# First weight chunk by single contraction columns, and the input by column pairs, at the head of a two-layer trunk

## What is computed

```python
def swiglu(x, w_gate, w_up, w_down):
    return (jax.nn.silu(x @ w_gate) * (x @ w_up)) @ w_down

def reference(x, ...):
    for l in range(DEPTH):
        x = layer_norm(ALPHA * x + 0.5 * swiglu(x, ffn1_w_gate[l], ffn1_w_up[l], ffn1_w_down[l]), ln1_g[l], ln1_b[l])
        mix = hybrid_mixer(x, w_in[l], ...)
        x = layer_norm(ALPHA * x + mix, ln2_g[l], ln2_b[l])
        x = layer_norm(ALPHA * x + 0.5 * swiglu(x, ffn2_w_gate[l], ffn2_w_up[l], ffn2_w_down[l]), ln3_g[l], ln3_b[l])
    return x
```

## Time and profile before

| | |
|---|---|
| median of 3 runs | 1088.04 us (1086.88 to 1088.79) |
| span of the profiled execution, first to last instruction | 1085.7 us |
| PE busy | 1073.1 us, 99% of the span |
| DVE busy | 768.2 us, 71% |
| ACT busy | 579.6 us, 53% |
| mean DMA rate over the span | 208 to 209 GB/s |

### The profile page before, as it was taken

One profiled execution on the slowest core, in us unless ns is written; L12 is line 12 of the kernel. 1 busy time (PEld: TensorE's weight loads), 2 busy tenths in 40 slices (PEclk: granted clock), 3 DMA queues, 4 the chain that ended last, 5 costly groups with the idle time before them and its releaser, 6 DMA issues.

```text
span 1085.7 us, 14631 instructions
## 1 busy us (share of the span) xinstructions
PE 1073.1 (99%) x5377; PEld 892.3 (82%) x5377; DVE 768.2 (71%) x764; ACT 579.6 (53%) x641; POOL 136.0 (13%) x137
## 2 busy tenths in 40 slices
PE   8999999999999999999999999999999999999996
PEld 6888888898888788888888888879978888888885
DVE  5756557789979775555779675666999787755556
ACT  5755554767554544444466565547774546444441
POOL 1497000000000000000007960000000000000000
PEclk9999999999999999999999999999999999999999
DMA  8877689355556477768648777675455674877770
GB/s 284 268 231 245 218 265 233 100 186 174 177 180 208 140 260 252 229 215 272 229 138 250 217 257 236 227 199 173 139 165 158 198 265 136 257 223 232 235 232 39
DMA packets 192369, 226.37 MB, mean 209 GB/s; under 512 B 31540, under 2 KB 157128, under 8 KB 192328
## 3 DMA queue, kind: packets, MB, share of 16 engines
q1 hardware_dynamic: 192328, 225.83, 65.7%
HBM read 214.26 MB, written 11.53 MB: 208 GB/s over the span
## 4 chain that ended last, share of the span: by engine, by line
PE 95%; DMA 2%; DVE 1%; SPq 1%; issue 1%; ACT 0%; POOLq 0%; DVEq 0%; POOL 0%
PE ps L572 25%; PE ps L549 18%; PE ps L551 18%; PE ps L550 18%; PE ps L533 2%; PE ps L534 2%; PE ps L535 2%; PE ps L920 1%; PE ps L922 1%; PE ps L921 1%; PE ps L587 1%; DMA raw<-in_ffn_w_up 1%; DMA raw<-in_w_in 1%; PE ps L850 1%; DMA tp<-in_ln_b 0%
## 5 line engine op out<-in xcount | busy, mean ns | idle before, releaser
L1387 DVE TENSOR_TENSOR w_lo<-raw,w_hi 128x2048 fp32r<-128x2048 f32 x173 | 403.7, 2338 | 171.1 <-ACT w_hi L1004 170.3
L1004 ACT CAST w_hi<-raw 128x2048 fp32r<-128x2048 f32 x173 | 330.1, 1911 | 174.5 <-PE ps L572 82.3
L549 PE MATMUL ps<-w_hi,xT 128*128 128x512 f32 x848 | 331.9, 391 | 0.4 <-DVE w_lo L1387 0.2
L551 PE MATMUL ps<-w_hi,xT 128*128 128x512 f32 x848 | 330.2, 389 | 0.0
L550 PE MATMUL ps<-w_lo,xT 128*128 128x512 f32 x848 | 330.2, 389 | 0.0
L549 PEld LDWEIGHTS ps<-w_hi,xT 128*128 128x128 f32 x848 | 159.2, 188 | 36.1 <-issue 2.4
L551 PEld LDWEIGHTS ps<-w_hi,xT 128*128 128x128 f32 x848 | 159.2, 188 | 33.2
L550 PEld LDWEIGHTS ps<-w_lo,xT 128*128 128x128 f32 x848 | 159.2, 188 | 32.6
L572 PE MATMUL ps<-w_hi,rows_hi 128*128 128x512 f32 x416 | 133.7, 393 | 0.0
L572 PE MATMUL ps<-w_hi,rows_lo 128*128 128x512 f32 x416 | 132.3, 390 | 0.0
L572 PE MATMUL ps<-w_lo,rows_hi 128*128 128x512 f32 x416 | 132.1, 390 | 0.0
(11 more groups left out here) (227 smaller groups left out, 1126.1 us busy)
## 6 DMA issues: line engine op xcount, KB each, us to landing
raw<-in_ffn_w_down SPq DMA_DIRECT2D x44, 1024.0 KB, 6.0
raw<-in_ffn_w_gate SPq DMA_DIRECT2D x86, 512.0 KB, 4.0
raw<-in_ffn_w_up SPq DMA_DIRECT2D x86, 512.0 KB, 5.1
raw<-in_w_in SPq DMA_DIRECT2D x30, 1024.0 KB, 5.1
hid_dram<-qT SPq DMA_DIRECT2D x160, 64.0 KB, 2.4
qT<-hid_dram SPq DMA_DIRECT2D x40, 256.0 KB, 2.7
raw<-in_w_out SPq DMA_DIRECT2D x8, 1024.0 KB, 5.0
raw<-in_w_in SPq DMA_DIRECT2D x8, 512.0 KB, 5.2
```

What stands on the lines that cost most here:

```text
L549: mm(o, xT[:, c, 0, tok], h, start=c == UPPER_FIRST[0], stop=False, skip_group_check=True)
L551: return mm(o, xT[:, c, 1, tok], h, start=False, stop=c == UPPER_FIRST[-1], skip_group_check=True)
L1004: nc.scalar.copy(w_hi[s][:, :], raw[s][:, :]).then_inc(hi_made.sem, 1)
L1387: tt(w_lo[s][:, :], raw[s][:, :], f32(w_hi[s][:, :]), ALU.subtract).then_inc(lo_made.sem, 1)
```

## The change

The input x is loaded in four pieces of two contraction columns: columns 4 and 5 of each token tile by themselves (load_rows), and the pairs 6 and 7, 0 and 1, 2 and 3 for both tiles at once (load_pair). The weights of chunks 0 and 1 come as eight columns, each with two transfers (gate and up, 128 KB each) and, but for the last of each chunk, a semaphore of its own. SP issues them in the order x 4-5 (two), column 5, x pair 1, columns 6 and 7, x pair 2, columns 0 and 1, x pair 3, columns 2 and 3; column 4 is issued by ACT ahead of its table load. ACT's casts and DVE's rests are made for one column or one pair at a time. PE makes the products of both tiles for one column after the other, and turns each pair of x one column ahead of the first product that needs it. The number of products is the same; five zero products stand at the start instead of six, and one instead of three behind the first turn. What follows chunk 1 is unchanged on every engine.

```diff
--- before.py
+++ after.py
@@ -199,8 +199,8 @@
             return ctx.enter_context(nc.semaphore(name))
 
         x_upper = [sem(f"x_upper{t}") for t in range(NT)]
-        x_lower = sem("x_lower")
-        first_landed, second_landed = sem("first_landed"), sem("second_landed")
+        x_pair = [None] + [sem(f"x_pair{p}") for p in (1, 2, 3)]
+        column_landed = {c: sem(f"column_landed{c}") for c in (4, 5, 6, 0, 1, 2)}
         third_hi, third_lo = sem("third_hi"), sem("third_lo")
         first_hi, first_lo = sem("first_hi"), sem("first_lo")
         small_landed, out_stored = sem("small_landed"), sem("out_stored")
@@ -231,7 +231,7 @@
         var_made = Events(sem("var_made"), 3 * NT)
         rstd_made = Events(sem("rstd_made"), 3 * NT)
         xn_made = Events(sem("xn_made"), 3 * 4)
-        tp_made = Events(sem("tp_made"), 3 * NT, before=NT)
+        tp_made = Events(sem("tp_made"), 3 * NT, before=3)
         tp_upper = Events(sem("tp_upper"), 3 * NT, before=NT)
         xTf_dve = Events(sem("xTf_dve"), 3 * 2)
         xTf_act = Events(sem("xTf_act"), 3 * 6)
@@ -304,25 +304,31 @@
 
             return slot[:, :].rearrange("p (c n) -> p c n", c=4)
 
+        def first_column(c):
+
+            for i, w in enumerate((ffn1_w_gate, ffn1_w_up)):
+                yield paired(raw[c < 4])[:, c % 4, i * 256:i * 256 + 256], w[0, c * P:c * P + P, 0:256]
+
         block = ctx.enter_context(nc.Block())
 
 
         @block.sync
         def _(sp):
-            first = [w[0].rearrange("(c p) n -> p c n", p=P) for w in (ffn1_w_gate, ffn1_w_up)]
-
-            def first_columns_of(c0, n, slot):
-
-                for i in range(2):
-                    yield (paired(raw[slot])[:, c0 % 4:c0 % 4 + n, i * 256:i * 256 + 256], first[i][:, c0:c0 + n, 0:256])
-
-            def load_upper(t):
-                sp.dma_start(xtok[:, t, D // 2:D], x[0, t * P:t * P + P, D // 2:D]).then_inc(x_upper[t], 16)
-
-            load_upper(0)
-            for dst, src in first_columns_of(4, 2, 0):
-                sp.dma_start(dst, src).then_inc(first_landed, 16)
-            load_upper(1)
+            def load_rows(t):
+                sp.dma_start(xtok[:, t, D // 2:D // 2 + 2 * P], x[0, t * P:t * P + P, D // 2:D // 2 + 2 * P]
+                             ).then_inc(x_upper[t], 16)
+
+            def load_pair(p):
+                n = slice(PAIRS[p][0] * P, PAIRS[p][1] * P + P)
+                sp.dma_start(xtok[:, :, n], x[0].rearrange("(t p) d -> p t d", p=P)[:, :, n]).then_inc(x_pair[p], 16)
+
+            def load_column(c):
+                for dst, src in first_column(c):
+                    sp.dma_start(dst, src).then_inc(column_landed[c], 16)
+
+            load_rows(0)
+            load_rows(1)
+            load_column(5)
             sp.sem_inc(lo_made.sem, SLOTS)
             sp.sem_inc(used.sem, SLOTS)
             def load(l, k, parts, slot=None):
@@ -367,12 +373,15 @@
 
                 k0 = FFN0[f]
                 if l == 0 and f == 0:
-                    load(l, k0, lambda r: first_columns_of(6, 2, 0))
-                    sp.dma_start(xtok[:, :, 0:D // 2], x[0].rearrange("(t p) d -> p t d", p=P)[:, :, 0:D // 2]
-                                 ).then_inc(x_lower, 16)
-                    for dst, src in first_columns_of(0, 2, 1):
-                        sp.dma_start(dst, src).then_inc(second_landed, 16)
-                    load(l, k0 + 1, lambda r: first_columns_of(2, 2, 1))
+                    load_pair(1)
+                    load_column(6)
+                    load(l, k0, lambda r: first_column(7))
+                    load_pair(2)
+                    load_column(0)
+                    load_column(1)
+                    load_pair(3)
+                    load_column(2)
+                    load(l, k0 + 1, lambda r: first_column(3))
                 else:
                     load(l, k0, gate_up(w_gate, w_up, l, 1, 0))
                     load(l, k0 + 1, gate_up(w_gate, w_up, l, 0, 0))
@@ -611,49 +620,63 @@
                     for _ in range(n):
                         mm(ps[:, 1, :], zero_b[:, 0:P], zero_b[:, :], start=True, stop=True, skip_group_check=True)
 
-                def turn(t, upper):
-
-                    for c in range(4):
-                        k = 4 * upper + c
-                        last = nc.tensor.transpose(ps[:, 6 - 2 * t + upper, c * P:c * P + P],
-                                                   xtok[:, t, k * P:k * P + P], ident[:, :])
-                    last.then_inc((tp_upper if upper else tp_made).sem, 1)
+                def turn_rows(t):
+
+                    pe.wait_ge(x_upper[t], 16)
+                    for n, c in enumerate(PAIRS[0]):
+                        last = nc.tensor.transpose(ps[:, 7 - 2 * t, n * P:n * P + P], xtok[:, t, c * P:c * P + P],
+                                                   ident[:, :])
+                    last.then_inc(tp_upper.sem, 1)
+
+                def turn_pair(p):
+
+                    pe.wait_ge(x_pair[p], 16)
+                    for n, c in enumerate(PAIRS[p]):
+                        for t in range(NT):
+                            at = n * SEQ + t * P
+                            last = nc.tensor.transpose(ps[:, (0, 6, 4, 7)[p], at:at + P], xtok[:, t, c * P:c * P + P],
+                                                       ident[:, :])
+                    last.then_inc(tp_made.sem, 1)
+
+                def both_tiles(c):
+
+                    hi, lo = (first_w_hi, first_w_lo) if c > 3 else (w_hi[0], w_lo[0])
+                    for t in range(NT):
+                        last = gate_up(hi, lo, t, c, t)
+                    return last
 
                 pe.wait_ge(zero_made, 1)
-                zeros(6)
+                zeros(5)
                 pe.wait_ge(ident_made, 1)
-                pe.wait_ge(x_upper[0], 16)
-                turn(0, 1)
-                zeros(3)
-                pe.wait_ge(x_upper[1], 16)
-                turn(1, 1)
+                turn_rows(0)
+                zeros(1)
+                turn_rows(1)
                 zeros(2)
+                pe.wait_ge(x_lo.sem, 1)
+                pe.wait_ge(first_lo, 1)
+                gate_up(first_w_hi, first_w_lo, 0, 4, 0)
                 pe.wait_ge(x_lo.sem, 2)
-                for c in (4, 5):
-                    pe.wait_ge(first_lo, c - 3)
-                    gate_up(first_w_hi, first_w_lo, 0, c, 0)
+                gate_up(first_w_hi, first_w_lo, 1, 4, 1)
+                turn_pair(1)
+                pe.wait_ge(first_lo, 2)
+                both_tiles(5)
                 pe.wait_ge(x_lo.sem, 4)
-                for c in (4, 5):
-                    gate_up(first_w_hi, first_w_lo, 1, c, 1)
-                pe.wait_ge(x_lower, 16)
-                turn(0, 0)
-                turn(1, 0)
                 pe.wait_ge(first_lo, 3)
-                for c in (6, 7):
-                    if c == 7:
-                        take(0, 0)
-                    for t in range(NT):
-                        last = gate_up(first_w_hi, first_w_lo, t, c, t)
-                last.then_inc(used.sem, 1)
+                both_tiles(6)
+                turn_pair(2)
+                take(0, 0)
+                both_tiles(7).then_inc(used.sem, 1)
+                pe.wait_ge(x_lo.sem, 6)
+                pe.wait_ge(first_lo, 4)
+                both_tiles(0)
+                turn_pair(3)
                 pe.wait_ge(second_lo.sem, second_lo.at(0, 0))
-                for upper in range(2):
-                    if upper:
-                        take(0, 1)
-                    for t in range(NT):
-                        pe.wait_ge(x_lo.sem, 6 + 2 * t)
-                        for c in (2 * upper, 2 * upper + 1):
-                            last = gate_up(w_hi[0], w_lo[0], t, c, t)
-                last.then_inc(used.sem, 1)
+                both_tiles(1)
+                pe.wait_ge(x_lo.sem, 8)
+                pe.wait_ge(first_lo, 5)
+                both_tiles(2)
+                take(0, 1)
+                both_tiles(3).then_inc(used.sem, 1)
 
             def third_of_input():
 
@@ -1118,28 +1141,38 @@
 
             def turn_input():
 
...
+                def rows_hi_(t):
+                    sc_.wait_ge(tp_upper.sem, t + 1)
+                    nc.scalar.copy(xT[:, 4:6, 0, t * P:t * P + P],
+                                   ps[:, 7 - 2 * t, 0:SEQ].rearrange("p (c n) -> p c n", c=2)).then_inc(x_hi.sem, 1)
+
+                def pair_hi(p):
+                    sc_.wait_ge(tp_made.sem, p)
+                    nc.scalar.copy(xT[:, PAIRS[p][0]:PAIRS[p][1] + 1, 0, :],
+                                   ps[:, (0, 6, 4, 7)[p], :].rearrange("p (c n) -> p c n", c=2)).then_inc(x_hi.sem, 2)
+
+                def column_hi(c, made, landed_, n):
+                    sc_.wait_ge(landed_, n)
+                    hi = first_w_hi if c > 3 else w_hi[0]
+                    nc.scalar.copy(paired(hi)[:, c % 4, :], paired(raw[c < 4])[:, c % 4, :]).then_inc(made, 1)
+
```

(46 more changed lines are left out.)

40 lines of the change are left out of this document (removed).

## The result

The changed kernel takes 1093.87 us (median of 6 runs, 1092.16 to 1096.14); the kernel before, run beside it, 1087.57 (1086.16 to 1090.10). The ratio is 1.0057, with a 95% interval of 1.0047 to 1.0067. Six more runs of the same program on another chip gave 1094.51 against 1088.75, 1.0053 (1.0036 to 1.0071). The forecast, 1090.7 with a range up to 1092.5, had the sign and the first part of the mechanism, but less than half of the size (+2.6 of +6.3 us).

A forecast was written before the change was run, and what follows sets the result against it. PE bounds the kernel (95% of the chain), so only the head matters, decided by lo_made of the second chunk. PE resuming at 28.28 instead of 25.64 gives +2.64 on 1088.04, so 1090.7 us; range 1088.4 to 1092.5.

The forecast's parts named there:

- First product: PE's first real product at the head: at 5.80 instead of 7.05, a gain of 1.25 us.
- column 4: Head transfers: x's first two pieces and column 4 of both weights landed at 4.4, with 4.0 and 5.0 as ends.
- its own sign: What the changed profile should show at the head: first product at 5.4 to 6.4.
- The gaps: PE stands 0.93 us at each of three x pairs, 2.8 in all, with one period of 4.30.
- Transfers hidden by the gaps: SP's 19 transfers up to column 3 instead of 11: last lands at 12.3 to 15.7, ACT asks at 17.7.
- lo_made and the down-chunk's load: Second chunk's rest on DVE made at 19.27 against 15.41; the down-load queued behind it on SP at 19.36.
- fourth chunk: PE goes on there at 28.28 instead of 25.64, +2.64 us, through norm rows landing at 25.62.
- The hidden rows' round trip through memory moves by about as much as PE, and had 0.9 us to spare: Behind the fourth chunk's start: the trip shifts along with PE; no cost of its own was added.
- 1: Norm rows land early, by 24.75, so PE's arrival decides: +1.6 to +1.8, 1089.7; chance 0.20.
- 2: No gap at the pairs: ACT and DVE turn one around within PE's 1.9 us; +0.3, 1088.4; chance 0.13.
- 3: Transfers bind the head: at 170 GB/s column 3 lands near 20.5; +5.2, 1093.3; chance 0.05.
- 4: Clock falls: gaps or fewer zero products leave the first 12 products slow; 2.4 more, 1093.1; chance 0.04.

The follow-up runs named there:

- Large transfers alone: Changed kernel with the transfers of before (x in three pieces, weights two columns at a time, all on SP); 1095.88 us, ratio 1.0055.
- only the late load: Kernel before, with SP holding the down-chunk's load until PE has used chunk 1; 1090.46 us, ratio 1.0032.
- all three edits: Changed kernel with weight column ahead of x pair on ACT and DVE, pairs turned earlier on PE, norm rows ahead of down-load; 1091.33 us, ratio 1.0024.
- large transfers with three edits: Kernel with all three edits, but with the transfers of before; 1088.40 us, ratio 1.0010.
- pairs turned earlier: Changed kernel with each pair of x turned about one column earlier on PE; 1089.77 us, ratio 1.0023.
- kernels without gaps and with small transfers: Changed kernel with weight column ahead of pair (1.0026), pairs turned earlier (1.0023), all three edits (1.0024), or these plus hidden rows out ahead of sixth chunk (1.0022).
- the control: Kernel before with the hidden rows' way out issued ahead of the sixth chunk in the first step of the first block; 1088.08 us, ratio 1.0006.
- filled kernel: Changed kernel with three zero products ahead of the first product and in each gap at the pairs; 1095.68 us, ratio 1.0061.
- second profile of the changed kernel: Changed kernel run and profiled again with no edit, on another chip; 1094.51 us, ratio 1.0053.

## Right and wrong, step by step

- *First product*, forecast 5.80, was 6.46. The wrong term was "column 4": I followed the weights' landing. They had landed by 4.6 (issued by ACT at 0.75 and 1.19, 3.2 and 3.4 us to landing), but ACT came to them only at 4.95: x landed at 3.85, its turn ran at 3.98, and ACT cast it at 4.68 ahead of the weights in its order. The chain of waits begins with x. Mis-sized by 0.66, just outside its own sign (5.4 to 6.4), and carried to all that follows.
- *The gaps*, 0.93 forecast, were 0.81 to 0.83. The period of 4.30 was 4.30 and 4.28 (10.77 to 15.07 to 19.35). Right.
- *Transfers hidden by the gaps*: right. Large transfers alone changed nothing, and without the gaps PE waited for the third chunk in three of four kernels with small pieces (1.38, 0.86, 0.20) and in neither with large ones. What this costs in time is not shown.
- *lo_made and the down-chunk's load*, 19.36 forecast, was 19.90; fourth chunk 28.28 forecast, was 29.13, +3.49 instead of +2.64. Of the 0.85, 0.54 came with the first product and the load; norm rows took 3.75 from the last issue instead of 3.47.
- *"The hidden rows' round trip through memory moves by about as much as PE, and had 0.9 us to spare"*: this step failed. PE was 3.49 late at the fourth chunk, the hidden rows 4.84 late on ACT, and the 0.9 to spare was gone. Their trip does not just move: SP was still at the sixth chunk's issue when they were ready (1.27), and the trip itself was longer (1.08). Its length is not fixed. It was 7.0 us before, 7.9 with only the late load, 8.1 after, 9.25 with all three edits. It is longest where the down-chunk's load (3.15 us ahead) and the sixth chunk's second half (0.6) are issued closest ahead of it, and shortest where that half is 1.7 or 2.3 ahead and was issued without a stall (before; large transfers with three edits). The distance from the down-chunk's load alone does not order the trips: 8.6 us at 5.7 with the pairs turned earlier, 7.9 at 5.0 with only the late load. How much each load adds is open. The trip became the chain at 35.31, 52.23 and 85.42, +1.75 in all, and the range had no room for it: 1088.04 + 3.49 alone would have been 1091.5, inside.
- *Rivals.* 1 fell (rows not early). 2 fell (the gaps are there); the kernels without gaps and with small transfers still were 2.4 to 2.8 us slower than before by the ratios, so "the whole gain of the head would be eaten by the load behind lo_made" held, with more behind it. 3 fell: the head moved 319 GB/s, and large transfers alone changed nothing. 4 fell for the gaps: the products behind them are at full spacing in every profile, and filling them gave nothing. Its other half, a head that starts at the slow spacing, came in some executions: not in the first profile of the changed kernel, but in its second (0.6 us) and in five others that start from it (some 0.5 to 2.1 us each). It is neither in the profile of before nor in that of the control, and one product long in that of the kernel with only the late load. Whether the fewer zero products at the start bring it, no run tests.

With the terms as measured the sum is 3.49 + 1.75 = 5.24 by 85 us, and 1088.04 + 5.24 = 1093.3, near the 1093.87 measured. Against the 1087.57 measured beside it, about 1 us stands in none of these terms; the slow products at the head can be a part of it.

No kernel here beats the one before. The best, with column order, large transfers and no gaps, is 0.1% behind it.

## What to carry to other kernels

When a queue carries both large loads and a short round trip that a later stage waits for, an event that moves one load later also shortens the distance between that load and the round trip, and so lengthens the trip (7.0 to 7.9 us where only that load, and with it what is queued behind it on SP, was held back); "it moves along with the rest" has to be costed with the bytes then ahead of it. Cutting a stage into finer steps turns each engine-to-engine latency into a gap unless the next step is started one step ahead. And a difference of two spans should be followed by the same instruction at several places, since one odd wait in either profile can hide or make up a microsecond or two.

## What the hardware showed unexpectedly

SP's issue of a transfer is 0.25 to 0.7 us, but can stall: the same small vector's issue took 1.37 us (before), 2.19 (after) and 2.91 (pairs turned earlier), and the sixth chunk's second one 1.58 instead of 0.46.

Behind longer stops PE ran products 0.43 us apart instead of 0.23 in some profiles. In the kernel with only the late load, after stops of 0.97 and 1.96 us, four products came at full spacing and the next eight did not; the stage there (us, busy PE, PEld, DVE, ACT, POOL, then the granted clock, DMA share, GB/s):

```profile
28.00:32.00 4.00, 3.15 (x10) 2.51 (x11) 3.00 (x2) 0.00 (x0) 0.00 (x0) 0.74 0.54 159
```

A granted clock of 0.74 mixes the two levels, 1.2 and 2.4 GHz. The filled kernel did the same after 1.77 us (0.60 from 31 to 35 us), but the early turns (1.96), all three edits (1.78) and the changed kernel (1.20) did not, and no gap of 0.8 us did. The Trainium skill (TensorE: Matmul & The Clock Gate, Part 1) has the clock fall after a window in which the engine idles; these rows show a fall behind some of the stops near 2 us and none behind others as long, so the length of the stop alone does not decide it here. At the head the granted clock reads 1.00 (5.0 to 8.0 us in the second profile of the changed kernel) although the spacing is the slow one, so there the spacing is the better sign.
